# A decoder step on one core: an expert's mixing begun in its own down phase, two pieces of the first and last group reordered, output stores merged and spread over two queues

## What is computed

```python
def hier_moe(h, w_rg, b_rg, w_re, b_re, w_gate, w_up, w_down):
    ...
    g_star = jnp.argmax(lg, axis=-1)
    ...
    top_p, top_i = lax.top_k(pe, TOP_K)
    w = p_group * top_p / jnp.sum(top_p, axis=-1, keepdims=True)
    ...
    y = grouped_experts(x, e_idx, w.astype(x.dtype), w_gate, w_up, w_down)

def expert_block(args):
    xblk, e = args
    return (jax.nn.silu(xblk @ w_gate[e]) * (xblk @ w_up[e])) @ w_down[e]
```

## Time and profile before

| | us |
|---|---|
| median of 3 runs (lowest, highest) | 1445.27 (1444.51, 1445.62) |
| time of the profiled execution | 1444.9 |
| its span, first to last instruction | 1443.1 |
| PE busy | 1259.4 (87%) |
| DVE busy | 450.6 (31%) |
| ACT busy | 223.4 (15%) |
| mean granted clock of PE, share of full | 0.959 |
| moved by DMA | 503.61 MB |

### The profile page before, as it was taken

One profiled execution on the slowest core, in us unless ns is written; L12 is line 12 of the kernel. 1 busy time (PEld: TensorE's weight loads), 2 busy tenths in 40 slices (PEclk: granted clock), 3 DMA queues, 4 the chain that ended last, 5 costly groups with the idle time before them and its releaser, 6 DMA issues.

```text
span 1443.1 us, 19987 instructions
## 1 busy us (share of the span) xinstructions
PE 1259.4 (87%) x8413; PEld 650.8 (45%) x8413; DVE 450.6 (31%) x887; ACT 223.4 (15%) x465; POOL 49.5 (3%) x36
## 2 busy tenths in 40 slices
PE   9999999999999998997787778787888777778777
PEld 7888888888788862222222122122222122122222
DVE  4322128674211043322321421232232232133132
ACT  3111232312000042110111011011001001011101
POOL 0000003141000001000000000000000000000000
PEclk9999999999999999998999998899899999899999
DMA  9965443659298349999999999999999999999997
GB/s 342 348 224 182 138 132 121 214 195 357 84 348 337 117 183 427 433 428 429 432 431 434 430 432 431 430 434 431 435 430 432 431 430 434 431 434 425 429 428 295
DMA packets 97601, 503.61 MB, mean 349 GB/s; under 512 B 5166, under 2 KB 75494, under 8 KB 81046
## 3 DMA queue, kind: packets, MB, share of 16 engines
q1 hardware_dynamic: 89746, 494.33, 84.4%
q10 hardware_dynamic: 7508, 8.06, 1.6%
q0 software_dynamic: 304, 0.61, 0.2%
HBM read 496.42 MB, written 6.59 MB: 349 GB/s over the span
## 4 chain that ended last, share of the span: by engine, by line
PE 55%; DMA 41%; DVE 2%; ACT 1%; issue 1%; SPq 1%; ACTq 0%; DVEq 0%
PE bank L695 30%; DMA ring<-in_w_gate 16%; DMA ring<-in_w_up 13%; DMA ring<-in_w_down 10%; PE bank L969 9%; PE bank L1009 4%; PE bank L909 2%; PE bank L1027 2%; DMA ring<-in_w_in 1%; PE bank L1024 1%; PE bank L1046 1%; DVE xa L1811 1%; PE bank L1040 1%; PE bank L986 0%; PE bank L786 0%
## 5 line engine op out<-in xcount | busy, mean ns | idle before, releaser
L969 PE MATMUL bank<-ring,bc 128*32 128x512 f32 x2048 | 272.3, 666 | 91.8 <-DMA ring<-in_w_gate 59.8
L695 PE MATMUL bank<-bc,ring 128*128 128x264 f32 x1536 | 350.9, 387 | 1.7 <-ACT cat L1177 1.3
L695 PEld LDWEIGHTS bank<-bc,ring 128*128 128x128 f32 x1536 | 288.1, 190 | 52.2 <-issue 2.3
L1811 DVE TENSOR_TENSOR xa<-xa,bank 128x512 f32<-128x512 f32 x192 | 119.8, 683 | 242.9 <-PE bank L1027 195.4
L969 PEld LDWEIGHTS bank<-ring,bc 128*32 128x32 f32 x2048 | 63.6, 118 | 268.1 <-issue 192.2
L695 PE MATMUL bank<-cat,ring 128*128 128x264 f32 x512 | 116.0, 387 | 0.0
L695 PEld LDWEIGHTS bank<-cat,ring 128*128 128x128 f32 x512 | 96.6, 190 | 19.0 <-issue 2.9
L1825 DVE COPY bc<-bank 128x512 f32<-128x512 f32 x32 | 22.1, 692 | 213.3 <-PE bank L969 213.3
L1009 PE MATMUL bank<-ring,cat 128*32 128x512 f32 x488 | 66.6, 666 | 20.0 <-DMA ring<-in_w_down 19.4
L909 PE MATMUL bank<-cat,bc 128*32 128x512 f32 x512 | 61.4, 597 | 13.5 <-DVE xa L1811 13.5
L1009 PE MATMUL bank<-ring,xa 128*32 128x512 f32 x512 | 61.4, 597 | 6.5 <-DVE bc L1828 3.3
(11 more groups left out here) (290 smaller groups left out, 986.3 us busy)
## 6 DMA issues: line engine op xcount, KB each, us to landing
ring<-in_w_gate SPq DMA_DIRECT2D x24, 4096.0 KB, 31.1
ring<-in_w_up SPq DMA_DIRECT2D x24, 4096.0 KB, 31.2
ring<-in_w_down SPq DMA_DIRECT2D x24, 4096.0 KB, 32.6
ring<-in_w_in SPq DMA_DIRECT2D x23, 2048.0 KB, 14.2
ring<-in_w_up SPq DMA_DIRECT2D x16, 2048.0 KB, 21.8
ring<-in_w_gate SPq DMA_DIRECT2D x15, 2048.0 KB, 30.1
ring<-in_w_down SPq DMA_DIRECT2D x13, 2048.0 KB, 29.8
ring<-in_w_out SPq DMA_DIRECT2D x8, 2048.0 KB, 16.6
```

Source lines behind the costliest of these rows:

```text
L695: m = pe.matmul(bank[n % 3][:, 0:T], w[:, k, (i % TPU) * P:(i % TPU + 1) * P], src[:, k, :], start=n_k == 0, stop=n_k == KT - 1)
L969: m = pe.matmul(bank[b][c * C:(c + 1) * C, :], xeT[j % 2][:, k, :], w[:, x, :], start=i == 0 and x < 4, stop=i == 1 and x >= 4, skip_group ...
L1811: V.tensor_tensor(xa[:, t, cols], xa[:, t, cols], bank[to[n]][:, :], ALU.add).then_inc(mix_added, 1)
```

## The change

On PE, in every group: the mixing of expert `j - 1` for tile 0 and the sample tile moves from expert `j + 1` (behind its first gate piece) to the end of expert `j`, right behind `down(j - 1, 1)`, with its waits for `ye_copied` and the others. `mix((1, j - 2))` moves from behind the second gate piece to ahead of it. DVE's adds move with them.

At the start of the first group, the first half's turning goes ahead of the sample tile's share of the second half's gather, and the second half's turning behind the first gate piece.

At the end of a group, `down(EG - 1, 0)` goes ahead of the last quarter of expert 2's tile 0, its sample tile and the turning of the last gates.

The stores of tiles 0 and 1 have two pieces of 1024 columns in place of four of 512, and two of the four sample stores move from SP to ACT.

```diff
-            for n in range(4):
-                added((0, last), n - 3)
-                cols = slice(512 * n, 512 * n + 512)
+            for n in range(2):
+                added((0, last), 2 * n - 2)
+                cols = slice(1024 * n, 1024 * n + 1024)
                 sp.dma_start(y[0][:, cols], xa[:, 0, cols]).then_inc(y_stored, 16)
             added((2, last), 0)
-            for n in range(4):
+            for n in range(2):
                 sp.dma_start(outs["y_sample"].rearrange("b o d -> b (o d)")[:, n * 512:(n + 1) * 512],
                              xa[n * C:n * C + NB, 2, 0:512]).then_inc(y_stored, 16)
-            sp.wait_ge(y_stored, 192)
+            sp.wait_ge(y_stored, 128)
...
-            def first_rows(half):
+            def first_rows(half, tiles):
-                for t in range(TT):
+                for t in tiles:
...
+            def turn_first(half):
                 pe.wait_ge(first_copied, half + 1)
                 for m_ in (2 * half, 2 * half + 1):
                     m = pe.transpose(bank[(5, 7)[half]][:, m_ * P:(m_ + 1) * P], xrow[:, m_ * P:(m_ + 1) * P], ident)
                 m.then_inc(xe_T, 1)
+            keep_busy(6)
+            first_rows(0, (0, 1, 2))
+            first_rows(1, (0, 1))
+            turn_first(0)
+            first_rows(1, (2,))
...
                         unit_products(j, "g", 0)
+                        if first:
+                            turn_first(1)
                         unit_products(j, "u", 0)
...
-                            pe.wait_ge(ye_copied, e - 1)
-                            pe.wait_ge(gateT_copied, e - 1)
-                            pe.wait_ge(act_ready, e)
-                            mix((0, j - 2))
-                            mix((2, j - 2))
+                            adds_done((0, j - 2))
+                            mix((1, j - 2))
                         unit_products(j, "g", 1)
                         if j == 1:
                             turn_hidden(e - 1)
                         if j >= 2:
-                            adds_done((0, j - 2))
-                            mix((1, j - 2))
                             adds_done((1, j - 2), -3)
...
                     down(j - 1, 1)
+                    if j < EG - 1:
+                        pe.wait_ge(xe_ready, 2 * e + 4)
+                        pe.wait_ge(gateT_copied, e)
+                        pe.wait_ge(act_ready, e + 1)
+                        pe.wait_ge(ye_copied, e)
+                        mix((0, j - 1))
+                        mix((2, j - 1))
...
-                adds_done((0, EG - 2), -2)
+                down(EG - 1, 0)
+                adds_done((0, EG - 2), -1)
                 mix_part((0, EG - 2), 3).then_inc(mixed, 1)
                 mix((2, EG - 2))
-                adds_done((0, EG - 2), -1)
                 turn_gate(EG - 1)
-                down(EG - 1, 0)
                 down(EG - 1, 1)
...
-            for n in range(4):
-                cols = slice(512 * n, 512 * n + 512)
-                act.wait_ge(row_moved, npass * (NG * 4) + (n + 1))
+            for n in range(2):
+                cols = slice(1024 * n, 1024 * n + 1024)
+                act.wait_ge(row_moved, npass * (NG * 4) + (2 * n + 2))
                 act.dma_start(y[1][:, cols], xa[:, 1, cols]).then_inc(y_stored, 16)
+            act.wait_ge(mix_added, npass * (NG * NADDS) + ADDS_BY[(2, EG - 1)])
+            for n in range(2, 4):
+                act.dma_start(outs["y_sample"].rearrange("b o d -> b (o d)")[:, n * 512:(n + 1) * 512],
+                              xa[n * C:n * C + NB, 2, 0:512]).then_inc(y_stored, 16)
...
-                        if j == 2:
-                            dve.wait_ge(x0_ready, 4)
...
-                            for t in (0, 2, 1):
...
-                                mix_adds((t, j - 2))
+                            mix_adds((1, j - 2))
...
+                        if 1 <= j < EG - 1:
...
+                            for t in (0, 2):
+                                mix_adds((t, j - 1))
```

More of the change, by code:

```diff
@@ L932, in first_rows @@
                                       skip_group_check=True)
-                m.then_inc(first_gathered, 1)
-            keep_busy(6)
-            first_rows(0)
-            first_rows(1)
-            for half in range(2):
+                if tiles[-1] == TT - 1:
+                    m.then_inc(first_gathered, 1)
+            def turn_first(half):
                 pe.wait_ge(first_copied, half + 1)
@@ L1814, in _ @@
                         e = it * EG + j
-                        if j == 2:
-                            dve.wait_ge(x0_ready, 4)
-                            dve.wait_ge(xs_moved, 4)
-                            dve.wait_ge(xa_ready, 4)
                         if j >= 2:
-                            for t in (0, 2, 1):
-                                if (t, j) == (1, 2):
-                                    dve.wait_ge(row_moved, it * 4 + 4)
-                                mix_adds((t, j - 2))
+                            if j == 2:
+                                dve.wait_ge(row_moved, it * 4 + 4)
+                            mix_adds((1, j - 2))
                         dve.wait_ge(u_done, e + 1)
@@ L1830, in _ @@
                         V.tensor_copy(actT[j % 2], bank[6][:, 0:P].rearrange("p (c s) -> p c s", c=FC)).then_inc(act_ready, 1)
+                        if 1 <= j < EG - 1:
+                            if j == 1:
+                                dve.wait_ge(x0_ready, 4)
+                                dve.wait_ge(xs_moved, 4)
+                                dve.wait_ge(xa_ready, 4)
+                            for t in (0, 2):
+                                mix_adds((t, j - 1))
                         if j == EG - 2:
```

## The result

| | before | changed |
|---|---|---|
| median of 12 runs each | 1444.45 us (1444.0 to 1445.73) | 1448.91 us (1446.02 to 1449.55) |
| ratio, 95% interval | | 1.0022 [1.0014, 1.003] |
| profiled execution | 1444.9 us, span 1443.1 | 1449.4 us, span 1447.6 |

The changed kernel is slower by 0.22% by the ratio and by 4.46 us (0.31%) from median to median, as its median falls into the upper of two groups of runs; 1443.9 and no change were forecast. The time lies above the range of 1442.0 to 1446.8. The two groups are five runs from 1446.02 to 1446.75 and seven from 1448.84 to 1449.55. The profiled one is of the upper group, so two things have to be found: what puts even the lower group 1.6 to 2.3 us above before's median, and what the other 2.6 us, from the middle of one group to that of the other, are.

A forecast was written before the change was run, and what follows sets the result against it. The weight stream was taken to bound 886 of 1443.1 us. Terms -0.5 + 0.9 - 0.7 - 1.1 = -1.4 us gave 1443.5 from 1444.9, 1443.9 on the median: no measurable change (chance 0.80), range 1442.0 to 1446.8.

The forecast's parts named there:

- the mixing ahead of piece 10: +0.9 us: First group: load 16 goes out 2.95 us later behind expert 0's mixing; 2.0 us is covered, 0.9 us comes through.
- The start, -0.5 us: Start of the weight stream: the earlier turning lets the load that restarts the stream go out 0.5 us sooner.
- the stream runs dry for the whole delay: Rival at load 16, first group: all 2.95 us of delay come through, giving 1445.9 us; chance 0.1.
- the clock falls in the tail: Rival at the last up piece: a PE wait of some 2.3 us lowers the clock, +1.5 us, 1445.4 us; chance 0.2.
- The stores, -1.1 us: Final stores: larger pieces and sample stores split over two queues end the kernel 1.1 us sooner.
- The rival that they give nothing: Final stores: bytes bound them and quicker issue is hidden; end at most 0.3 us sooner, 1444.7 us; chance 0.1.
- The tail on PE, -0.7: Last group: `down(3, 0)` fills the 0.53 us wait for DVE, and 0.14 us comes from mixings leaving; -0.7 us.
- Groups 1 to 6 and piece 11: 0: Moved mixing and adds fall where PE waits for weights, and piece 11's load has more cover; both cost 0.
- (1): Sign at the stream's start: the restarting load is issued 0.5 us earlier against the first gather.
- (3): Sign in the tail: the last up piece begins when it lands, behind a DMA wait of about 2.3 us.
- (2): Sign behind piece 10: load issued about 2.5 us later, landing in 7 to 7.5 us; GB/s dips near 570.
- (5): Sign at the stores: two stores of 1024 columns on each queue, and SP's last issue before 1439.5 us.

The follow-up runs named there:

- the two other profiles above: Profiles of the kernel before with the moved mixing alone (median 1447.89 us), and of the changed kernel with expert 0's mixing put back behind piece 10 (1444.04 us).

## Why the prediction was wrong

**The step that failed is the term "the mixing ahead of piece 10: +0.9 us".** The delay of the issue was right (2.95 predicted, 3.03 measured), and so were the 7.3 us of the load. Wrong was the cover of 2.0 us: it was counted from load 15's *last* landing, 572.15. The last part of a load comes 1.78 us behind its first in the running stream (570.33 and 572.11), and only 0.38 behind it once the queue has run dry (578.44 and 578.82). Those 1.4 us look like time won, but they come back: load 18 of the changed kernel already has 1.7 us between its parts again (588.22 to 589.92). By first landings the cover is 0.7 us. Counted from the first gathering, load 16's last part came 1.00 us later than before, as forecast (0.9), but its first part 2.40 us later, and by load 18 the last part was 2.3 us late too. "All later landings move by it" is what did not hold: they moved by the delay of the first part. The term was 3.03 - 0.7 = +2.3, not +0.9, and the moved mixing alone lost 2.44. This lies inside the ends of 0 and 2.95 that the prediction gave the term; the value taken between them was wrong. Why the last parts close up behind a dry queue and fall back later is not shown.

The 6.8 us that the prediction estimates beside it is worked out from a section of the Trainium skill (page "DMA: Bandwidth & Descriptors", "Anatomy of one DMA") on transfers that GpSimd issues. These loads are issued by SP, and into a dry queue they took 7.21 to 7.35 us in five profiles.

**The start, -0.5 us**, came at the restarting load, 0.56, and at load 15, 0.61. But in the changed kernel it is worth nothing: load 16 is issued when PE has used piece 10, and PE reaches it 3.03 us later counted from the first gathering, early start or not. Start and mixing together give -0.61 + 2.94 = +2.33 us, that is nearly the whole delay less the 0.7 of cover. The two terms were added as if they were independent.

**Rival "the stream runs dry for the whole delay"** (chance 0.1, 1445.9) was near what happened. What I held against it, 4.4 us of data in flight, was the last landing again.

**Rival "the clock falls in the tail"** (0.2, +1.5 us) happened too, in the profiled execution, with 3.50 us for the piece, 1.57 more; the seven of twelve runs in the upper group say that it was no exception. It costs more where it reaches the folds and the residual, as in the two other profiles above. The forecast had the wait right (2.3 us, measured 2.40) and took one of two outcomes for the likely one. With both rivals true at once the sum is my own -0.5 + 2.95 - 0.7 - 1.1 + 1.5 = 2.15. The two profiled executions differ by 4.5. Of the 2.35 that are missing, the stores are 1.28 (-1.1 forecast, +0.18 measured), the early fall of the clock 0.82, and the tail on PE 0.25.

**The stores, -1.1 us, measured +0.2** in the profile and +0.4 alone (1444.72 against 1444.33, an interval that holds zero). The rival that they give nothing held. SP's issue did shrink, 3.34 to 1.57 us. But before, the last landing came 1.6 us behind the end of SP's last issue, and now it comes 3.5 behind: the bytes set the end, at 372 to 399 GB/s. They nearly did so before: the DMA share was 1.03 at 378 GB/s from 1436 to 1440 us, of which the earlier trace rows showed the first half. The 0.6 us by which the first store starts later eats what the rate gives. The Trainium skill, page "DMA: Bandwidth & Descriptors", section "Issuing engines are not separate DMA queues", says that a second issuing engine saves issue time alone; that is what the runs show here, and I gave it 0.1.

**The tail on PE, -0.7**: -0.45 in the profile; the wait for DVE went as predicted. **Groups 1 to 6 and piece 11: 0** was right: the stream lost nothing beyond load 16 (2.94 us, where load 16's lead gives 2.92), though load 18 went out at 577.07 in place of 571.62 (before).

In what was to show the steps, (1), (3) and (4) came; (2) came with 3.03 for 2.5 us; of (5) the split came, and SP's last issue ended 7.13 us behind the start of ACT's copy in place of 8.90, but the last landing did not follow. Both signs of a wrong forecast came: the stream took 2.94 us more, where 1 was the bound, and the stores ended 0.18 us later behind the last add, where at least 0.3 sooner was asked.

## What to carry to other kernels

In a ring of buffers, measure how early each load is issued against the *first* landing of the load before it, at the one place where it is smallest. Here a lead of 1.9 us was needed and 2.6 were there, so of PE work ahead of that piece all that goes beyond 0.7 us goes straight to the end, and it also takes back what was won earlier. A wait that the trace already shows to cost clock is to be counted as an outcome with its own share of the runs, not as a rival against the sum. Work that has to fill such a wait must be sized by what it takes where it stands. And before two profiles are set against each other, look in both for a fallen clock ahead of the change: here it was 0.8 us of 4.5.

## What the runs showed of the hardware

- Matmuls of one shape (128x32 by 128x512) took 0.85 us each when all went to one quarter of the array's columns (6.60 us and a last record of 0.59 for eight), and 0.23 us each when four went to four quarters (1.90 us for eight): 3.6 times. The two kinds differ also in which slices of `xeT` they read. The Trainium skill, page "TensorE: Matmul & The Clock Gate", section on packing small matmuls, has matmuls of few columns run at the same time in distinct column groups; these runs agree.
- The last of a 2 MiB load's 16 parts landed 1.6 to 2.1 us behind its first at load 15 (fifteen profiles) and 0.3 to 0.5 behind it at the load that found a dry queue (five profiles), and one or two loads later the lag was back at 1.7 to 1.9. By the last 1 MiB piece it had grown to 3.2 to 3.8 us, in one profile to 4.6.
- Behind a wait of 2.35 to 2.41 us the granted clock stood at 0.50 for 3.4 us in one profile and for 6.8 in two; the time from the weights' last landing to the stores' last landing was 14.39 us in the changed kernel's profile and 15.87 and 15.65 in those two, against 13.10 before.
- A clock fallen for 3.4 us at 13.7 us made a stretch of 64 matmuls take 16.16 us in place of 14.48, in two of fifteen profiles, with no change to the code there.
